# Four raw weight buffers shared by two phases, first loads of the channel mixer issued inside mixing, and two token differences on VectorE

## The chip, the core and the metric

The kernel runs on one core of a Trainium2 chip. The time is that of the device in microseconds, from the first to the last instruction, as the median of several runs. The engines work in parallel, each through its own list of instructions, and meet only at semaphores: TensorE (PE, matmuls), VectorE (DVE), ScalarE (ACT), GpSimd (POOL) and SyncE (SP), which here only issues transfers between device memory and the on-chip memory.

## What is computed

One layer of a transformer in float32 on 2048 tokens of width 1024. The change lies in its second half, which starts when the outputs of the two groups of attention heads, `o_dsa` and `o_nsa`, are in device memory:

```
mixed = jnp.concatenate([group_rms(o_dsa), group_rms(o_nsa)], axis=-1) * mix_gain
h = layer_norm(ALPHA * x + mixed @ w_out, ln1_g, ln1_b)
ffn = (jax.nn.silu(h @ w_gate) * (h @ w_up)) @ w_down
return layer_norm(ALPHA * h + ffn, ln2_g, ln2_b)
```

`w_out` is 1024 x 1024, `w_gate` and `w_up` are 1024 x 2816, `w_down` is 2816 x 1024.

## The kernel before

The program runs five phases one after the other: projection, compression, attention, mixing (`mixing_phase`) and the channel mixer (`ffn_phase`). A phase ends in a barrier of all engines, which SP reaches when its last stores have landed; the next phase uses the same on-chip memory for other tiles.

Every float32 product is made of three: an operand is split into a high part (a copy by ScalarE into a reduced format, `w_hi`, `x_hi`, `ot_hi`) and a low part (raw minus high, by VectorE, `w_lo`, `x_lo`, `ot_lo`), and TensorE adds hi x hi, hi x lo and lo x hi.

**Mixing** takes 16 tiles of 128 tokens. For a tile, ScalarE squares the attention output `o_in` (`square`), GpSimd makes the inverse root (`rinv`), VectorE scales (`scale`, which multiplies by the gain too), TensorE turns the tile (`turn_o`), ScalarE and VectorE split it (`high`, `low`), and TensorE multiplies it with `w_out` (`project`, 48 matmuls of 512 columns). VectorE adds `x` (`add_x`) and takes the moments, then come GpSimd's root, ScalarE's `norm`, VectorE's `gains`, GpSimd's addition of the offset (`add_b`, L1927, into `ho`), TensorE's `turn_h` and ScalarE's `copy_h`. SP stores `ho` to `h` and the turned tile to `h_t` (`store`). `o_in`, `x_in`, `ho` and `ht` have two buffers each; `add_b` of tile t waits until the store of tile t - 2 has landed. Tile 0 is special: its products follow the eight row blocks of `w_out` as they are split (`follow_weights`), and these come through two raw buffers, `w_raw`: the load of block k waits for w_lo of block k - 2. SP issues in the order in which its code is written: identity, gain, `ln_g` and `ln_b` broadcast, o tiles 0 and 1, the eight weight blocks, x tiles 0 and 1, o tile 2. VectorE and TensorE wait for all four of the small loads at their start.

**The channel mixer** multiplies by a scheme with 7 products in place of 8 for each 2 x 2 blocks (`ORDER = 7`), over two groups of 1024 tokens. A set n is the 7 products of two blocks of 128 columns of `w_gate` (even n) or `w_up` (odd n). The weight operands are raw blocks or sums of them in `st` (`sums`, four per set, on GpSimd), and the x operands are raw blocks or differences of them (`turn_x`, numbers 0 to 3, each in halves r = 0 and 1). The x operands are made once per group. For group 0 the blocks lie in `gs` (block 0), `y` (blocks 1 and 3, and 2 in the buffer of block 1) and the differences t2 in `lnp`. ScalarE and VectorE go through the products j = 0 to 6 in order, each with two x halves of 1024 columns and one weight part of 512, and TensorE waits for the low parts of both:

```
 for j in range(ORDER):
     for r in range(2):
         low_x(0, r, j)
     low(0, 0, j)
```

GpSimd's list at the start is: sum 0, differences 0 and 1, sums 1 and 2, difference 2, sum 3, difference 3. A product j uses: x block 0 and raw weights (j = 0), difference 1 and sum 2 (1), difference 2 and sum 1 (2), difference 0 and sum 0 (3), x block 2 (4), difference 3 (5), x block 3 and sum 3 (6). SP's first requests are the weights of set 0, x blocks 0, 1 and 3, the weights of set 1, and, once x_lo has gone through three products, x block 2 into the buffer that block 1 had.

## Time and profile before

| | us |
|---|---|
| median of 3 runs | 3850.33 (3845.58 to 3852.93) |
| the profiled execution | 3852.21 |
| its span, first to last instruction | 3850.4 |
| TensorE busy in it | 3510.7 (91%) |
| VectorE busy | 2376.6 (62%) |
| ScalarE busy | 1796.1 (47%) |
| GpSimd busy | 1251.5 (33%) |
| mixing starts | 2205.0 |
| channel mixer starts | 2460.8 |

Times in the trace count from the start of the span. A timeline lists instructions in order of time, with neighbours of one kind merged (x2, x8) and, in brackets, how long the engine was idle before and which instruction or transfer ended that. A duration given for merged instructions is that of all of them together. The granted clock is the share of TensorE's full clock, 2.4 GHz, that it had.

### The profile page before, as it was taken

How to read it: one execution, taken by the hardware profiler on the slowest of the kernel's cores; microseconds unless marked ns; L12 is line 12 of the kernel's file. 1: busy time of each engine (PE TensorE's matmuls, PEld its weight loads, DVE VectorE, ACT ScalarE, POOL GpSimd, SP SyncE). 2: the span in 40 equal slices, each digit the busy share in tenths (PEclk: the TensorE clock that was granted, in tenths of full speed). 3: DMA queues.
4: the chain of work that ended last, by engine and by line, in shares of the span. 5: the costliest groups of instructions: out<-in, count | busy, mean ns of one | idle time of the engine just before them, and what ended most of it. 6: DMA issues, size and time to landing. Idle time of an engine off the chain costs nothing. (4 is left out here: it accounts for less than half of the span.)

```text
span 3850.4 us, 55869 instructions
## 1 busy us (share of the span) xinstructions
PE 3510.7 (91%) x19064; PEld 2999.8 (78%) x19064; DVE 2376.6 (62%) x5054; ACT 1796.1 (47%) x3061; POOL 1251.5 (33%) x1951
## 2 busy tenths in 40 slices
PE   6999757989898999999989889599999999999997
PEld 6999646878787888888868768478888888888876
DVE  9999245666666667766774244476564666666354
ACT  3333125666666776776677333233332333333232
POOL 5454024444443333323322023433231235332031
PEclk9999769999999999999899989799999999999998
DMA  4343220000000000000000045332224452322344
GB/s 145 117 144 120 70 52 27 24 17 16 16 16 16 16 13 11 9 14 5 7 9 4 34 154 163 131 110 80 92 81 148 166 178 77 110 99 85 140 142 148
DMA packets 189764, 289.62 MB, mean 75 GB/s; under 512 B 33458, under 2 KB 129842, under 8 KB 189490
## 3 DMA queue, kind: packets, MB, share of 16 engines
q1 hardware_dynamic: 188004, 283.97, 22.0%
q8 instruction: 150, 2.46, 0.3%
q10 hardware_dynamic: 1488, 2.20, 0.2%
q14 instruction: 122, 1.00, 0.1%
HBM read 211.15 MB, written 74.97 MB: 74 GB/s over the span
## 5 line engine op out<-in xcount | busy, mean ns | idle before, releaser
L1459 ACT ACTIVATE a_p_t<-a_ps_st 128x512 f32<-128x512 f32 x716 | 437.7, 615 | 370.8 <-PE a_ps_st L1349 192.3
L2482 PE MATMUL f_ps<-f_x_hi,f_w_hi 128*128 128x512 f32 x1232 | 482.7, 392 | 37.2 <-DVE f_w_lo L2603 37.2
L1466 ACT ACTIVATE a_junk_a<-a_index,a_tk 128x384 bf16<-128x384 f32 (+13 forms) x336 | 445.2, 1325 | 112.2 <-DVE a_halves L1576 56.1
L2482 PE MATMUL f_ps<-f_x_lo,f_w_hi 128*128 128x512 f32 x1232 | 481.8, 391 | 0.0
L2482 PE MATMUL f_ps<-f_x_hi,f_w_lo 128*128 128x512 f32 x1232 | 481.6, 391 | 0.0
L1375 PEld LDWEIGHTS a_ps_o<-a_vsl,a_p_t 128*128 128x128 f32 x2176 | 316.9, 210 | 25.4 <-DVE a_fin L1673 2.3
L1180 POOL TENSOR_SCALAR a_tk<-a_tk,a_halves 128x1 f32<-128x1 f32 x336 | 104.0, 309 | 630.0 <-ACT a_junk_a L1466 628.8
L1375 PE MATMUL a_ps_o<-a_vsl,a_p_t 128*128 128x65 f32 x2176 | 299.9, 285 | 1.4 <-DVE a_fin L1673 1.4
L2482 PEld LDWEIGHTS f_ps<-f_x_hi,f_w_hi 128*128 128x128 f32 x1232 | 232.9, 189 | 87.5 <-DVE f_w_lo L2603 39.2
L1375 PEld LDWEIGHTS a_ps_o<-a_dv,a_p_t 128*128 128x128 f32 x2176 | 288.6, 193 | 8.8
L2502 PE MATMUL f_ps<-f_w_hi 128*128 128x512 f32 x704 | 275.1, 391 | 4.8 <-DVE f_w_lo L2613 4.8
L2502 PE MATMUL f_ps<-f_w_lo,f_w_hi 128*128 128x512 f32 x704 | 274.2, 389 | 0.0
L2502 PE MATMUL f_ps<-f_w_hi,f_w_lo 128*128 128x512 f32 x704 | 274.0, 389 | 0.0
L1375 PE MATMUL a_ps_o<-a_dv,a_p_t 128*128 128x65 f32 x2176 | 272.8, 269 | 0.0
L289 PE MATMUL p_ps<-pw_hi,px_hi 128*128 128x384 f32 (+1 forms) x672 | 228.0, 339 | 47.0 <-DVE pw_lo L395 29.5
L2482 PEld LDWEIGHTS f_ps<-f_x_hi,f_w_lo 128*128 128x128 f32 x1232 | 232.7, 189 | 48.9
L2482 PEld LDWEIGHTS f_ps<-f_x_lo,f_w_hi 128*128 128x128 f32 x1232 | 232.8, 189 | 48.0
L2609 DVE TENSOR_TENSOR f_w_lo<-f_raw,f_w_hi 128x1024 fp32r<-128x1024 f32 x88 | 121.3, 1378 | 240.7 <-ACT f_w_hi L2537 240.7
L2527 ACT ACTIVATE f_w_hi<-f_st 128x512 fp32r<-128x512 f32 x176 | 110.7, 632 | 309.7 <-PE f_ps L2482 293.9
L2537 ACT ACTIVATE f_w_hi<-f_raw 128x1024 fp32r<-128x1024 f32 x88 | 93.4, 1061 | 330.7 <-PE f_ps L2502 316.9
L1556 DVE SCALAR_TENSOR_TENSOR a_index<-a_relu,a_iw,a_index 128x512 f32<-128x512 f32 (+3 forms) x266 | 179.7, 716 | 97.3 <-ACT a_relu L1453 95.0
L289 PE MATMUL p_ps<-pw_lo,px_hi 128*128 128x384 f32 (+1 forms) x672 | 225.8, 336 | 0.0
(327 smaller groups left out, 8467.1 us busy)
## 6 DMA issues: line engine op xcount, KB each, us to landing
f_raw<-in_w_down SPq DMA_DIRECT2D x88, 512.0 KB, 3.3
px_raw<-in_x_t SPq DMA_DIRECT2D x48, 512.0 KB, 4.4
f_raw<-in_w_gate SPq DMA_DIRECT2D x44, 512.0 KB, 4.7
f_raw<-in_w_up SPq DMA_DIRECT2D x44, 512.0 KB, 4.5
g_scratch<-f_gs SPq DMA_DIRECT2D x22, 1024.0 KB, 7.5
f_raw<-g_scratch SPq DMA_DIRECT2D x88, 256.0 KB, 3.4
z_scratch<-p_z SPq DMA_DIRECT2D x16, 768.0 KB, 3.4
o_scratch<-a_oacc SPq DMA_DIRECT2D x32, 256.0 KB, 2.1
```

The lines of the kernel that those rows point to most:

```text
L289: mm = pe.matmul(bank[n % 8][:, 0:w], xs[:, j, k * P:(k + 1) * P], ws[:, j, k, 0:w], start=(k == 0 and i == 0), stop=(j not in (0, 3) and ...
L1180: last = mine(pool.tensor_scalar(moved, cnt, (t + 1) * P - 2 * TOPK + 0.5, halves[:, m:m + 1], ALU.is_le, ALU.mult))
L1375: mm = pe.matmul(ps_o[n % 2][:, h * cols:(h + 1) * cols], p_t[:, s % PT_RING, h * P:(h + 1) * P], v, start=(j == 0 and h == 0), stop=(j == ...
L1459: act.activation(p_t[:, s % PT_RING, :], ps_st[s % ST_BANKS][:, :], ACT.Exp, scale=SCALE).then_inc(exp_done, 1)
L1466: act.activation(junk_a[:, 0:w], index[t % 2][:, 0:w], ACT.Sign, bias=thr, scale=-1.0, accum_out=cnt).then_inc(counted, 1)
L1556: dve.scalar_tensor_tensor(dst, relu[:, r % RELU_RING, 0:w], weight, dst, ALU.mult, ALU.add).then_inc(index_done, 1)
L2482: mm = pe.matmul(out[:, :], w[:, j, k * P:(k + 1) * P], x[:, j, k], start=(k == 0 and i == 0), stop=(k == 3 and i == 2))
L2502: mm = pe.matmul(acc(G, a)[:, :], x[:, s + 2, cols], w[:, s + half, :], start=(f == 0 and i == 0), stop=(f == FT - 1 and i == 2))
L2527: act.activation(slot(w_hi, j), source(m, j), ACT.Copy).then_inc(hi_done, 1)
L2537: act.activation(w_hi[:, s:s + 2], raw[:, 2 * (F % 2)].rearrange("p (a n) -> p a n", a=2), ACT.Copy).then_inc(hi_done, 1)
L2609: dve.tensor_tensor(w_lo[:, s:s + 2], raw[:, 2 * (F % 2)].rearrange("p (a n) -> p a n", a=2), w_hi[:, s:s + 2].bitcast(F32), ALU.subtract) ...
```

## The change

The four raw weight buffers of the channel mixer (`raw`), its buffers `gs` and `y`, and the semaphores of their loads are now made before mixing and held through both phases. Mixing uses the four `raw` buffers for `w_out` in place of its own two; the load of block k waits for w_lo of block k - 4. SP's first requests in mixing come in another order, and the waits for small loads are parted in two: gain and identity, and the two layer norm vectors.

At mixing's step 13 of 16, SP issues seven requests of the channel mixer: the weights of sets 0 and 1, and x blocks 0, 1 and 3, each x block as one transfer of 1 MB where there were two. Their tiles of `h_t` are 0 to 7, whose stores SP waits for. The mixer's phase itself requests only x block 2 at its start, into `uu`, with no wait.

In the channel mixer the differences 0 and 1 of group 0 are made by VectorE, after its part for j = 0, and GpSimd starts with sums 0, 1 and 2. No matmul and no split is added or removed.

```diff
-        w_raw = sb("m_w_raw", [P, 2, D_MODEL])
...
-            for dst, src in ((ident, ident_in), (gain_b, gain.broadcast_to([P, D_MODEL])),
-                             (g_b, ln_g.broadcast_to([P, D_MODEL])), (b_b, ln_b.broadcast_to([P, D_MODEL]))):
-                sp.dma_start(dst[:, :], src).then_inc(small_ld, 16)
+            def load_w(k):
+                if k >= 4:
+                    sp.wait_ge(w_lo_done, k - 3)
+                sp.dma_start(raw[:, k % 4], w_rows[k]).then_inc(w_ld[k % 4], 16)
+
             for t in range(2):
                 load_o(t, t)
-            for k in range(KT):
-                if k >= 2:
-                    sp.wait_ge(w_lo_done, k - 1)
-                sp.dma_start(w_raw[:, k % 2], w_rows[k]).then_inc(w_ld[k % 2], 16)
-            for t in range(2):
-                load_x(t, t)
-
+            for dst, src in ((ident, ident_in), (gain_b, gain.broadcast_to([P, D_MODEL]))):
+                sp.dma_start(dst[:, :], src).then_inc(gain_ld, 16)
+            for k in range(3):
+                load_w(k)
+            load_x(0, 0)
+            load_w(3)
             load_o(2, 0)
+            load_w(4)
+            load_x(1, 1)
+            load_w(5)
+            for dst, src in ((g_b, ln_g.broadcast_to([P, D_MODEL])), (b_b, ln_b.broadcast_to([P, D_MODEL]))):
+                sp.dma_start(dst[:, :], src).then_inc(small_ld, 16)
+            for k in range(6, KT):
+                load_w(k)
...
+                if isinstance(t, int) and t == TILES - 3:
+                    for b in range(2):
+                        sp.wait_ge(ht_out[b], 16 * (GROUP // P // 2))
+                    for dst, src, landed in ffn_first:
+                        sp.dma_start(dst, src).then_inc(landed, 16)
...
-            pe.wait_ge(small_ld, 64)
+            pe.wait_ge(gain_ld, 32)
...
-                act.wait_ge(w_ld[k % 2], 16 * (k // 2 + 1))
-                act.activation(w_hi[:, k], w_raw[:, k % 2], ACT.Copy).then_inc(w_hi_done, 1)
+                act.wait_ge(w_ld[k % 4], 16 * (k // 4 + 1))
+                act.activation(w_hi[:, k], raw[:, k % 4], ACT.Copy).then_inc(w_hi_done, 1)
...
-                dve.wait_ge(small_ld, 64)
+                dve.wait_ge(small_ld, 32)
...
-            dve.wait_ge(small_ld, 64)
+            dve.wait_ge(gain_ld, 32)
...
+def ffn_first_loads(h_t, w_gate, w_up, raw, gs, y, raw_ld, x_ld):
+    w_cols = [w.rearrange("(k p) n -> p k n", p=P) for w in (w_gate, w_up)]
+    xt_rows = h_t.rearrange("(k p) n -> p k n", p=P)
+
+    def weights(m, half):
+        return raw[:, 2 * m + half].rearrange("p (k n) -> p k n", k=4), w_cols[m][:, 4 * half:4 * half + 4, 0:2 * P], raw_ld[2 * m + half]
+
+    def tokens(dst, n):
+        return dst, xt_rows[:, 4 * (n // 2):4 * (n // 2) + 4, (n % 2) * PART:(n % 2 + 1) * PART], x_ld[n]
+
+    return [weights(0, 0), tokens(gs[:, :, :], 0), weights(0, 1), tokens(y[:, 0:2].rearrange("p t (k n) -> p (t k) n", k=2), 1),
+            tokens(y[:, 2:4].rearrange("p t (k n) -> p (t k) n", k=2), 3), weights(1, 0), weights(1, 1)]
...
-                late = y[:, r, :].rearrange("p (k n) -> p k n", k=2)
-                return (gs[:, ks], late, late, y[:, 2 + r, :].rearrange("p (k n) -> p k n", k=2),
+                return (gs[:, ks], y[:, r, :].rearrange("p (k n) -> p k n", k=2), uu[:, 2 + 2 * r:4 + 2 * r], y[:, 2 + r, :].rearrange("p (k n) -> p k n", k=2),
...
-                for part in ((0, 1) if G == 0 else (r,)):
-                    sp.dma_start(x_blocks(G, part)[block_no], xt_rows[:, k0 + 2 * part:k0 + 2 * part + 2, col:col + PART]).then_inc(x_ld[block_no], 16)
+                if G == 0:
+                    sp.dma_start(uu[:, 2:6], xt_rows[:, k0:k0 + 4, col:col + PART]).then_inc(x_ld[block_no], 16)
+                else:
+                    sp.dma_start(x_blocks(G, r)[block_no], xt_rows[:, k0 + 2 * r:k0 + 2 * r + 2, col:col + PART]).then_inc(x_ld[block_no], 16)
...
-            load_set(0, 0)
-            for block_no in (0, 1, 3):
-                load_x(0, None, block_no)
-            load_set(0, 1)
-            sp.wait_ge(x_lo_done, 6)
             load_x(0, None, 2)
...
+        def turn_x(eng, G, r, n):
+
+            b11, b12, b21, b22, t2 = x_blocks(G, r)
+            ld = 16 * (1 if G == 0 else 2 + r)
+            if n == 0:
+                eng.wait_ge(x_ld[1], ld)
+                eng.wait_ge(x_lo_done, x_number(G, r, 0) + 1)
+                op = eng.tensor_tensor(b11, b12, b11, ALU.subtract)
+            elif n == 1:
+                eng.wait_ge(x_ld[3], ld)
+                eng.wait_ge(t_done, t_number(G, r, 0) + 1)
+                op = eng.tensor_tensor(t2, b22, b11, ALU.subtract)
+            elif n == 2:
+                eng.wait_ge(t_done, t_number(G, 1 if G == 0 else r, 1) + 1)
+                op = eng.tensor_tensor(b12, b22, b12, ALU.subtract)
+            else:
+                eng.wait_ge(x_ld[2], ld)
+                eng.wait_ge(x_lo_done, x_number(G, r, 1) + 1)
+                op = eng.tensor_tensor(t2, b21, t2, ALU.subtract)
+            op.then_inc(t_done, 1)
...
-            sums(0, 0, (0,))
+            sums(0, 0, (0, 1, 2))
             for r in range(2):
-                turn_x(0, r, 0)
-            for r in range(2):
-                turn_x(0, r, 1)
-            sums(0, 0, (1, 2))
-            for r in range(2):
-                turn_x(0, r, 2)
+                turn_x(pool, 0, r, 2)
             sums(0, 0, (3,))
             for r in range(2):
-                turn_x(0, r, 3)
+                turn_x(pool, 0, r, 3)
...
+                if j == 0:
+                    for n in range(2):
+                        for r in range(2):
+                            turn_x(dve, 0, r, n)
```

On SP at the start of mixing (`m_` names are mixing's tiles, `f_` names the channel mixer's, `m_o_in` an attention tile, `m_x_in` an x tile, `in_w_out` the weights), before:

```order
L1880 DMA m_ident<-in_consts 128x128
L1880 DMA m_gain<-in_gain 128x1024
L1880 DMA m_ln_g<-in_ln_g 128x1024
L1880 DMA m_ln_b<-in_ln_b 128x1024
L1866 DMA m_o_in<-o_scratch 128x1024 x2
L1886 DMA m_w_raw<-in_w_out 128x1024 x2
L1886 DMA m_w_raw<-in_w_out 128x1024 [waits m_w_lo_done] x6
L1870 DMA m_x_in<-in_x 128x1024 x2
L1866 DMA m_o_in<-o_scratch 128x1024 [waits m_scaled] x2
```

and in the changed kernel:

```order
L1867 DMA m_o_in<-o_scratch 128x1024 x2
L1887 DMA m_ident<-in_consts 128x128
L1887 DMA m_gain<-in_gain 128x1024
L1882 DMA f_raw<-in_w_out 128x1024 x3
L1871 DMA m_x_in<-in_x 128x1024
L1882 DMA f_raw<-in_w_out 128x1024
L1867 DMA m_o_in<-o_scratch 128x1024 [waits m_scaled]
L1882 DMA f_raw<-in_w_out 128x1024 [waits m_w_lo_done]
L1871 DMA m_x_in<-in_x 128x1024
L1882 DMA f_raw<-in_w_out 128x1024 [waits m_w_lo_done]
L1897 DMA m_ln_g<-in_ln_g 128x1024
L1897 DMA m_ln_b<-in_ln_b 128x1024
```

The o tiles and the gain now stand first, and x and o tiles stand between the weight blocks, of which only the last four wait. On SP at the end of mixing and the start of the channel mixer (`h_scratch` and `ht_scratch` are `h` and `h_t`), before:

```order
L1874 DMA h_scratch<-m_ho 128x1024 [waits m_h_done]
L1876 DMA ht_scratch<-m_ht 128x8x128 [waits m_ht_done]
L1874 DMA h_scratch<-m_ho 128x1024 [waits m_h_done]
L1876 DMA ht_scratch<-m_ht 128x8x128 [waits m_ht_done]
L1769 UNCONDITIONAL_BRANCH [waits m_h_out1,m_ht_out1,m_ht_out0,m_h_out0]
L2264 UNCONDITIONAL_BRANCH [waits barrier_Pool_Activation_PE_DVE_SP_release]
L2271 DMA f_raw<-in_w_gate 128x4x256 x2
L2294 DMA f_gs<-ht_scratch 128x2x512 x2
L2294 DMA f_y<-ht_scratch 128x2x512 x4
L2271 DMA f_raw<-in_w_up 128x4x256 x2
L2294 DMA f_y<-ht_scratch 128x2x512 [waits f_x_lo_done]
L2294 DMA f_y<-ht_scratch 128x2x512
```

and now, from the store of h_t tile 12 on:

```order
L1877 DMA ht_scratch<-m_ht 128x8x128 [waits m_ht_done]
L1912 DMA f_raw<-in_w_gate 128x4x256 [waits m_ht_out1,m_ht_out0]
L1912 DMA f_gs<-ht_scratch 128x4x512
L1912 DMA f_raw<-in_w_gate 128x4x256
L1912 DMA f_y<-ht_scratch 128x4x512 x2
L1912 DMA f_raw<-in_w_up 128x4x256 x2
L1875 DMA h_scratch<-m_ho 128x1024 [waits m_h_done]
L1877 DMA ht_scratch<-m_ht 128x8x128 [waits m_ht_done]
L1875 DMA h_scratch<-m_ho 128x1024 [waits m_h_done]
L1877 DMA ht_scratch<-m_ht 128x8x128 [waits m_ht_done]
L1875 DMA h_scratch<-m_ho 128x1024 [waits m_h_done]
L1877 DMA ht_scratch<-m_ht 128x8x128 [waits m_ht_done]
```

The requests for `f_raw`, `f_gs` and `f_y` moved from behind the barrier to a place ahead of the stores of tiles 13 to 15. On GpSimd at the start of the channel mixer, before:

```order
L2375 TENSOR_TENSOR f_st<-f_raw 128x512 [waits f_raw_ld1,f_raw_ld0,f_fixed_set]
L2393 TENSOR_TENSOR f_gs<-f_y,f_gs 128x1024 [waits f_x_lo_done,f_x_ld1] x2
L2397 TENSOR_TENSOR f_lnp<-f_y,f_gs 128x1024 [waits f_t_done,f_x_ld3] x2
L2377 TENSOR_TENSOR f_st<-f_raw 128x512
L2380 TENSOR_TENSOR f_st<-f_st,f_raw 128x512 [waits f_s_done]
L2399 TENSOR_TENSOR f_y<-f_y 128x1024 x2
L2383 TENSOR_TENSOR f_st<-f_raw,f_st 128x512 [waits f_s_done,f_lo_done]
L2403 TENSOR_TENSOR f_lnp<-f_y,f_lnp 128x1024 [waits f_x_lo_done,f_x_ld2] x2
```

and in the changed kernel:

```order
L2415 TENSOR_TENSOR f_st<-f_raw 128x512 [waits f_raw_ld1,f_raw_ld0,f_fixed_set]
L2417 TENSOR_TENSOR f_st<-f_raw 128x512
L2420 TENSOR_TENSOR f_st<-f_st,f_raw 128x512 [waits f_s_done]
L2390 TENSOR_TENSOR f_y<-f_y 128x1024 [waits f_t_done] x2
L2423 TENSOR_TENSOR f_st<-f_raw,f_st 128x512 [waits f_s_done,f_lo_done]
L2394 TENSOR_TENSOR f_lnp<-f_u,f_lnp 128x1024 [waits f_x_lo_done,f_x_ld2] x2
```

The pairs on `f_gs` and the first on `f_lnp` are gone from GpSimd. They stand on VectorE now, behind its part for j = 0:

```order
L2632 TENSOR_TENSOR f_x_lo<-f_gs,f_x_hi 128x1024 [waits f_x_hi_done] x2
L2618 TENSOR_TENSOR f_w_lo<-f_raw,f_w_hi 128x512 [waits f_hi_done]
L2383 TENSOR_TENSOR f_gs<-f_y,f_gs 128x1024 [waits f_x_lo_done,f_x_ld1] x2
L2387 TENSOR_TENSOR f_lnp<-f_y,f_gs 128x1024 [waits f_t_done,f_x_ld3] x2
L2632 TENSOR_TENSOR f_x_lo<-f_lnp,f_x_hi 128x1024 [waits f_x_hi_done] x2
L2618 TENSOR_TENSOR f_w_lo<-f_st,f_w_hi 128x512 [waits f_hi_done]
```

## Rows read from the trace of the kernel before

**Rows 1.** Windows of three stretches: busy time (instructions) of each engine, granted clock, DMA share, GB/s.
```profile
2205.00:2245.00 40.00, 18.52 (x60) 13.03 (x61) 13.83 (x14) 12.62 (x19) 2.60 (x7) 0.67 0.63 223
...
2444.00:2520.00 76.00, 30.43 (x107) 23.34 (x106) 41.53 (x31) 24.81 (x32) 38.43 (x24) 0.66 0.35 119
2520.00:3850.00 1330.00, 1300.44 (x5725) 1073.55 (x5723) 768.92 (x983) 435.00 (x635) 366.51 (x269) 0.99 0.34 119
```

**Rows 2.** Timeline of the SP queue, mixing's start: start, duration, engine, line, operation, out<-in, count.
```profile
2205.00 0.34 SPq L1880 DMA_DIRECT2D m_ident<-in_consts  x1
...
2208.12 28.52 SPq L1886 DMA_DIRECT2D m_w_raw<-in_w_out  x8
...
2237.63 0.91 SPq L1866 DMA_DIRECT2D m_o_in<-o_scratch  x2
```

**Rows 3.** Transfers from 2205 to 2245 us: rate in 40 slices of 1 us; median us to landing.
```profile
GB/s 4 172 254 262 422 328 340 418 426 406 438 254 12 0 0 0 0 0 37 303 283 225 201 0 115 381 66 369 119 0 258 266 184 385 381 184 311 418 414 303
...
m_w_raw<-in_w_out SPq DMA_DIRECT2D x8, 512.0 KB, 3.3
```

**Rows 4.** Timeline, ScalarE at mixing's start; in brackets the idle time before and its releaser.
```profile
2213.84 0.63 ACT L2014 ACTIVATE m_junk<-m_o_in 128x512 f32<-128x512 f32 x1 [15.36 <-DMA m_o_in<-o_scratch]
...
2220.61 1.99 ACT L2045 ACTIVATE m_w_hi<-m_w_raw 128x1024 fp32r<-128x1024 f32 x2
...
2244.70 0.63 ACT L2014 ACTIVATE m_junk<-m_o_in 128x512 f32<-128x512 f32 x1 [4.16 <-DMA m_o_in<-o_scratch]
```

**Rows 5.** Timeline, VectorE at mixing's start.
```profile
2216.58 1.42 DVE L2067 SCALAR_TENSOR_TENSOR m_on<-m_o_in,m_rinv,m_gain 128x512 f32<-128x512 f32 x2 [14.53 <-POOL m_rinv L1934]
...
2240.58 1.23 DVE L2102 TENSOR_TENSOR m_w_lo<-m_w_raw,m_w_hi 128x1024 fp32r<-128x1024 f32 x1 [0.85 <-ACT m_w_hi L2045]
```

**Rows 6.** Timeline, TensorE where mixing's third tile is transposed.
```profile
2250.01 1.94 PE L1956 MATMUL m_t_o<-m_ident,m_on 128*128 128x128 f32 x8 [4.32 <-DVE m_ot_lo L2072]
```

**Rows 7.** Timeline of the SP queue, mixing's end and the channel mixer's start.
```profile
2427.69 0.39 SPq L1876 DMA_DIRECT2D ht_scratch<-m_ht  x1
...
2460.82 0.95 SPq L2271 DMA_DIRECT2D f_raw<-in_w_gate  x2
```

**Rows 8.** Transfers from 2460 to 2480 us: rate in 40 slices of 0.5 us.
```profile
GB/s 0 0 0 27 160 291 344 383 391 385 293 225 201 283 352 406 410 389 381 414 401 410 410 385 393 389 379 375 367 346 352 352 322 219 51 2 0 0 0 0
```

**Rows 9.** Timeline, ScalarE, then VectorE, at the channel mixer's start.
```profile
2469.80 2.00 ACT L2549 ACTIVATE f_x_hi<-f_gs 128x1024 fp32r<-128x1024 f32 x2 [12.70 <-DMA f_gs<-ht_scratch]
...
2470.88 2.36 DVE L2617 TENSOR_TENSOR f_x_lo<-f_gs,f_x_hi 128x1024 fp32r<-128x1024 f32 x2 [18.86 <-ACT f_x_hi L2549]
2473.16 2.83 DVE L2603 TENSOR_TENSOR f_w_lo<-f_raw,f_w_hi 128x512 fp32r<-128x512 f32 x1
...
2495.56 0.68 DVE L2603 TENSOR_TENSOR f_w_lo<-f_st,f_w_hi 128x512 fp32r<-128x512 f32 x1
```

**Rows 10.** Timeline, GpSimd, mixing's last addition and the channel mixer's start.
```profile
2452.10 2.34 POOL L1927 TENSOR_TENSOR m_ho<-m_hn,m_ln_b 128x1024 f32<-128x1024 f32 x1 [2.61 <-DVE m_hn L2094]
...
2466.07 1.26 POOL L2375 TENSOR_TENSOR f_st<-f_raw 128x512 f32<-128x512 f32 x1 [5.09 <-DMA f_raw<-in_w_gate]
2472.56 5.64 POOL L2393 TENSOR_TENSOR f_gs<-f_y,f_gs 128x1024 f32<-128x1024 f32 x2 [5.23 <-DMA f_y<-ht_scratch]
2478.17 4.68 POOL L2397 TENSOR_TENSOR f_lnp<-f_y,f_gs 128x1024 f32<-128x1024 f32 x2
...
2500.80 5.67 POOL L2403 TENSOR_TENSOR f_lnp<-f_y,f_lnp 128x1024 f32<-128x1024 f32 x2 [6.25 <-DMA f_y<-ht_scratch]
```

**Rows 11.** Timeline, TensorE, the channel mixer's first products.
```profile
2476.05 0.80 PE L2482 MATMUL f_ps<-f_x_hi,f_w_hi 128*128 128x512 f32 x1 [19.58 <-DVE f_w_lo L2603]
...
2509.29 0.80 PE L2482 MATMUL f_ps<-f_x_hi,f_w_hi 128*128 128x512 f32 x1 [7.11 <-DVE f_w_lo L2603]
2509.89 0.63 PE L2482 MATMUL f_ps<-f_x_lo,f_w_hi 128*128 128x512 f32 x1
2510.31 0.63 PE L2482 MATMUL f_ps<-f_x_hi,f_w_lo 128*128 128x512 f32 x1
```

## What the change will do to the time

> **What bounds the kernel now.** I read the windows by stage first [rows 1]. In the channel mixer's long stretch, 2520 to 3850 us, TensorE is busy 1300 of 1330 us at a granted clock of 0.99: nothing there can be hidden further, and the change leaves its work alone. The two stretches in front of it are different. From 2205 to 2245 us TensorE is busy 18.5 of 40 us, and from 2444 to 2520 us 30.4 of 76 us, at granted clocks of 0.67 and 0.66. Both are starts of a phase, where every engine waits for first loads and first preparations. So I ask only how much earlier the steady work of each phase begins, and carry the difference to the end of the program.
>
> Next come the timelines of the two starts. In mixing, ScalarE waits 15.36 us for the first attention tile, whose load is issued behind four others [rows 2, 4]. Then two raw buffers make each weight load wait for the VectorE subtraction that frees its buffer, so the eight loads take 28.5 us to issue [rows 2], and the eighth w_lo starts at 2240.58 and ends at 2241.8 [rows 5]. Last of all comes the load of token tile 2, issued at 2237.63 behind the weights [rows 2]; ScalarE idles 4.16 us for it until 2244.70 [rows 4], and the chain from there (root, scaling, low part) lets TensorE transpose tile 2 at 2250.01 [rows 6]. After that TensorE has only small gaps. In the channel mixer, nothing is requested before 2460.82 [rows 7]; the first x arrives at 2469.80 [rows 9]; then GpSimd works through four turned x halves, and TensorE's first product starts at 2476.05 and its last wait ends at 2509.29 [rows 11].
>
> **Part 1, the first loads of mixing.** By the transfer rates [rows 3], bytes flow after about 2206 at 250 to 430 GB/s; from 2205.0 to 2213.84 the queue brought identity, three broadcasts and the first o tile, 0.06 + 4 x 0.524 = 2.16 MB. At the 400 GB/s of the full slices a 0.524 MB transfer takes 1.3 us, and 3.3 us from issue to landing alone [rows 3], so about 2 us are fixed. From the new order I get these landings: o0 2209.3, o1 2210.5, gain 2211.5, w0 2212.8, w1 2214, w2 2215.2, x0 2216.5, w3 2217.7, o2 2219. Between the start of squaring and of scaling lie 2216.58 - 2213.84 = 2.74 us [rows 4, 5]; scaling of tile 0 then starts at 2212.05, 4.5 us earlier. The gain is there by then, and VectorE now waits only for it and the identity.
>
> **Part 2, four buffers.** The first w_hi moves by the same 4.5 us from 2220.61 [rows 4] to 2216.1. With w0 to w3 landed, ScalarE makes one each 1.0 us (two took 1.99) and VectorE one w_lo each 1.2 us [rows 4, 5]: w_lo(0) ends at 2218.4, w_lo(3) at 2221.9. The loads w4 to w7 are issued as w_lo(0) to w_lo(3) end. They land behind the interleaved x1 and the two broadcasts: w4 2221.7, w5 2224.2, w6 2227.9, w7 2229.2. That is the transfer bound: 16 tiles and the identity, 8.45 MB, at 400 GB/s take 21 us and with the fixed part end near 2229. The last w_lo ends 1.05 + 1.2 us plus a queue step later, at 2231.6, against 2241.8. TensorE finishes tile 0 at about 2233.1.
>
> **Part 3, tile 2 early.** o2 landed long ago, so ScalarE squares it right after the last w_hi (2230.4 to 2232.1), GpSimd takes the root, VectorE scales by 2234.8. The turn of tile 1 follows the weight products (2233.1 to 2234.9), its high halves end at 2235.5, its low halves at 2236.2, and TensorE turns tile 2 at 2236.3, where it did at 2250.01 [rows 6]. **Gain 13.7 us.** The 4.16 us idle for o2 is in it. The extra waits on SP (o2 between w3 and w4) are on scaled tiles that are done by then; queued behind them are only loads that I have counted.
>
> **Part 4, the mixer's first loads near mixing's end.** Seven requests are put on SP after the store of h_t tile 12, which was issued at 2427.69 [rows 7]; with everything shifted I keep the old times for this part. They carry four weight halves of 0.524 MB and three x blocks of 1.05 MB, 5.24 MB, exactly what the old start fetched. That took from 2460.82 to about 2477.4 [rows 7, 8], 16.6 us, so they land at about 2446 with the store in front. The SP wait ahead of them is for h_t stores of tiles 0 to 7, long done. What is queued behind them is the store of h tile 13; GpSimd's addition of tile 15 needs it, since it reuses that buffer, and starts at 2452.10 [rows 10]. Expected landing 2448 to 2449, so it is hidden with 3 us to spare, at no cost.
>
> **Part 5, the mixer's start.** The phase still begins at 2460.8, since the old waits on all stores stay. ScalarE no longer waits until 2469.80, GpSimd not until 2466.07 [rows 9, 10]. Block 2 of x alone is requested there, into its own buffer, lands near 2466, and is needed at 2484. It was late before: GpSimd waited 6.25 us for it until 2500.80 [rows 10], because its buffer had to be freed first.
>
> The price of each step: a 1024 column w_lo or x_lo step 1.18 us on VectorE, a 512 column one 0.62 to 0.68 [rows 9]; on GpSimd 2.34 and 1.26 [rows 10]. The two do not overlap: a 512 column subtraction took 2.83 us beside GpSimd's subtractions [rows 9], and GpSimd's pair took 5.64 us, where the next pair took 4.68 [rows 10]. I therefore lay the steps of both engines one after the other, alternating where both are ready. With this rule the old start comes out within 0.1 us of the start of the second weight set on TensorE (2519.6: 2509.29 plus one product at half clock and two at full), so I trust it.
>
> New chain: three token sums on GpSimd interleave with two x_lo and w_lo(0); first product 2468.1 (was 2476.05). The four subtractions moved to VectorE cost 4 x 1.16 = 4.6 us there and end at 2472.7; on GpSimd they took 2472.56 to 2482.85, 10.3 us [rows 10]. Then, each with GpSimd's 2.35 us steps between: w_lo(1) 2480.4, w_lo(2) 2486.9, w_lo(3) 2492.2, w_lo(4) 2497.6, w_lo(5) 2500.6, w_lo(6) 2503.5. A product of 12 matmuls lasts 12 x 0.232 = 2.8 us at the full clock [rows 1]. The last one starts at 2503.6, and the second set at 2506.3, against 2519.6. **Gain 13.3 us.** What is late next is VectorE's chain of subtractions, no longer a load.
>
> **Sum.** The profiled execution took 3852.2 us (span 3850.4), 1.9 us above the median of the three runs, 3850.3. 13.7 + 13.3 = 27.0 us off give 3825.2 in that execution, 3823.3 at the median. I take 3824, since rounding of the landings tends to come out late.
>
> **Bounds of the unknown terms.** (a) Transfer rate in mixing's start: at the 330 GB/s that I get from 5.24 MB in 16 us [rows 8], the 8.45 MB end 4.6 us later, and the gain is 9.1 instead of 13.7; above 430 GB/s no slice goes [rows 3], which gives 1.5 us more. (b) Clock: a matmul that follows idle time is spaced 0.43 us instead of 0.23 [rows 11], 2.4 us for a product. The short gaps of the new start could leave TensorE at 1.2 GHz in its last product before the steady stretch, at up to 2.4 us, or save about as much, since the 7 us gap before 2509.29 goes. (c) The four moved subtractions, if GpSimd's own step gets in between each pair: at most two steps of 2.35 us, 4.7.
>
> **Rivals.** *The transfers are the bound of mixing's start*, term (a) in full: 3824 + 5 = 3829. For it speaks that now 16 tiles want to come in 24 us; against it that slices beyond 400 GB/s stand in both windows of transfers [rows 3, 8].
>
> *The h store waits behind the early loads.* In the old start the data arrived in the order of the requests: weights for 2466.07, x for 2469.80, the next x for 2472.56 [rows 9, 10]. If 5.24 MB move at only 250 GB/s beside mixing's own traffic, they take 21 us, h tile 13 lands at about 2454, GpSimd's last addition starts 2 to 6 us late, and TensorE's last turn and the phase's end with it: 3826 to 3830. The Trainium skill, "DMA: Bandwidth & Descriptors", section "Queues, rings and completion order", says that a DMA engine consumes the descriptors of one ring in ring order; by that rule the store cannot overtake the loads at all, which speaks against this placement. The order of arrival named above agrees.
>
> *Slower than before.* The same mechanism decides it: h tile 13 would have to land later than 2452.1 + 27 = 2479 us, so that more than 51 us pass from the requests. At 100 GB/s, 5.24 MB take 52 us and the store ends at 2483: about 3860 with the block's end pushed by 31 against 27 saved, plus waits of the h_t store behind it. Nothing in the rows goes so slow over 16 us.
>
> *The change doesn't do what it says*: mixing is held elsewhere and only the mixer's start gains (3837), or the reverse. For mixing the likeliest holder is TensorE at half clock through the weight products, which would make them 2.55 us each where VectorE delivers one each 1.2: last product 2238, gain 9.
>
> **How the numbers follow.** Forecast as summed, 3818 to 3829: 0.68. Transfer bound 3829 to 3832: 0.10. Store behind the loads: 0.08. One of the starts alone, 3834 to 3843: 0.08. Something off both starts eats it, within 0.2% of before: 0.04. Slower: 0.02. 0.2% or 7.7 us is what a measurement of this kernel can tell from no change. The range 3816 to 3836 leaves out 2 in 10 at most. Faster 0.94, same 0.04, slower 0.02.
>
> **What would show it.** In the profile after: TensorE turns mixing's tile 2 at 2235 to 2238; ScalarE idles for weights once or twice, near w6; o2 causes no wait. GpSimd's last addition in mixing follows VectorE, not a DMA. In the channel mixer the first product comes 7 to 8 us after the phase's start instead of 15.2, VectorE's moved subtractions take 1.2 us each, and the last TensorE wait before the steady stretch ends 37 to 43 us after the phase's start instead of 48.5. The stretch behind it is as long as before. Wrong would be: a w_lo(7) after 2236, a wait of GpSimd for the h store, or a steady stretch that grew.

## The result, and the profile after

| | before | changed |
|---|---|---|
| median of 5 runs, us | 3851.83 (3845.58 to 3853.34) | 3825.56 (3818.74 to 3828.66) |
| profiled execution | 3852.21 | 3825.56 |
| its span | 3850.4 | 3823.8 |

The ratio is 0.9929, with a 95% interval of 0.9918 to 0.994: 26.3 us faster. The forecast was 3824, range 3816 to 3836. The total is right; its two halves are not, as the rows show, and their errors cancelled.

Windows of the changed kernel, in the columns of [rows 1]:

```profile
2205.00:2245.00 40.00, 21.85 (x85) 17.48 (x86) 18.98 (x22) 14.52 (x24) 3.85 (x13) 0.71 0.67 241
2444.00:2520.00 76.00, 54.88 (x211) 42.67 (x210) 66.40 (x60) 33.26 (x47) 39.17 (x23) 0.80 0.20 67
2507.00:3824.00 1317.00, 1286.48 (x5664) 1062.07 (x5662) 758.68 (x968) 427.42 (x622) 360.55 (x264) 0.99 0.35 119
```

TensorE is busy 21.85 of the first 40 us (18.52 before) and 54.88 us of the 76 around the mixer's start (30.43 before). In the long stretch nothing of note changed: TensorE idles 30.5 of 1317 us, before it was 29.6 of 1330. For sharper numbers I split the end of the program in two. **Mixing's length** runs from SP's first request of mixing to the first instruction of the channel mixer: 255.8 us before (2205.00 to 2460.82), 244.6 after (2205.30 to 2449.90), **11.2 less**. **The mixer's length** runs from there to the end of the span: 1389.6 before, 1373.9 after, **15.7 less**. Their sum, 26.9, is the gain in the profiled spans (26.6) but for the start of mixing, 0.3 us later.

Timelines at mixing's start, changed kernel: SP's queue, ScalarE, VectorE, TensorE (columns as in [rows 2] and [rows 4]).

SP's queue:

```profile
2205.30 0.82 SPq L1867 DMA_DIRECT2D m_o_in<-o_scratch  x2
...
2206.64 0.43 SPq L1887 DMA_DIRECT2D m_gain<-in_gain  x1
...
2214.92 0.33 SPq L1867 DMA_DIRECT2D m_o_in<-o_scratch  x1
...
2222.31 1.26 SPq L1882 DMA_DIRECT2D f_raw<-in_w_out  x2
```

ScalarE:

```profile
2208.58 0.63 ACT L2028 ACTIVATE m_junk<-m_o_in 128x512 f32<-128x512 f32 x1 [9.80 <-DMA m_o_in<-o_scratch]
...
2231.65 1.06 ACT L2059 ACTIVATE m_w_hi<-f_raw 128x1024 fp32r<-128x1024 f32 x1 [4.22 <-DMA f_raw<-in_w_out]
```

VectorE:

```profile
2213.48 2.74 DVE L2081 SCALAR_TENSOR_TENSOR m_on<-m_o_in,m_rinv,m_gain 128x512 f32<-128x512 f32 x4 [11.13 <-DMA m_gain<-in_gain]
...
2232.74 2.49 DVE L2116 TENSOR_TENSOR m_w_lo<-f_raw,m_w_hi 128x1024 fp32r<-128x1024 f32 x2 [4.05 <-ACT m_w_hi L2059]
```

TensorE:

```profile
2234.02 0.50 PE L1991 MATMUL m_y<-m_w_hi,m_ot_hi 128*128 128x512 f32 x1 [3.47 <-DVE m_w_lo L2116]
...
2238.46 1.04 PE L1970 MATMUL m_t_o<-m_ident,m_on 128*128 128x128 f32 x8
2241.16 1.07 PE L1970 MATMUL m_t_o<-m_ident,m_on 128*128 128x128 f32 x8 [1.66 <-DVE m_ot_lo L2086]
```

Compare [rows 4 to 6]. The first attention tile is squared 3.3 us after SP's first request instead of 8.8. VectorE then idles for the gain until 2213.48. ScalarE waits 4.22 us for weight block 6, TensorE 3.47 us for its low part, and tile 2 is turned at 2241.16 (2250.01 before).

At mixing's end and the mixer's start, changed kernel: SP's queue; GpSimd; VectorE; TensorE; and, from two views of transfers, the time to landing of the `h` store requested at 2425.78 and of the two early loads of `w_up`.

SP's queue:

```profile
2421.75 3.98 SPq L1912 DMA_DIRECT2D f_raw<-in_w_up  x2
2425.78 2.58 SPq L1875 DMA_DIRECT2D h_scratch<-m_ho  x1
```

GpSimd:

```profile
2441.19 2.34 POOL L1941 TENSOR_TENSOR m_ho<-m_hn,m_ln_b 128x1024 f32<-128x1024 f32 x1 [2.61 <-DVE m_hn L2108]
2449.90 0.10 POOL L2400 MEMSET f_power<- 128x1 f32 x1 [6.37 <-POOLq L1770]
...
2450.14 1.27 POOL L2415 TENSOR_TENSOR f_st<-f_raw 128x512 f32<-128x512 f32 x1
```

VectorE:

```profile
2454.62 1.74 DVE L2618 TENSOR_TENSOR f_w_lo<-f_raw,f_w_hi 128x512 fp32r<-128x512 f32 x1
2456.29 2.35 DVE L2383 TENSOR_TENSOR f_gs<-f_y,f_gs 128x1024 f32<-128x1024 f32 x2
2458.56 2.35 DVE L2387 TENSOR_TENSOR f_lnp<-f_y,f_gs 128x1024 f32<-128x1024 f32 x2
2460.90 4.51 DVE L2632 TENSOR_TENSOR f_x_lo<-f_lnp,f_x_hi 128x1024 fp32r<-128x1024 f32 x2
2465.33 2.82 DVE L2618 TENSOR_TENSOR f_w_lo<-f_st,f_w_hi 128x512 fp32r<-128x512 f32 x1
...
2486.62 0.68 DVE L2618 TENSOR_TENSOR f_w_lo<-f_raw,f_w_hi 128x512 fp32r<-128x512 f32 x1
2487.22 2.35 DVE L2632 TENSOR_TENSOR f_x_lo<-f_y,f_x_hi 128x1024 fp32r<-128x1024 f32 x2
2489.49 0.68 DVE L2618 TENSOR_TENSOR f_w_lo<-f_st,f_w_hi 128x512 fp32r<-128x512 f32 x1
```

TensorE:

```profile
2456.42 0.79 PE L2497 MATMUL f_ps<-f_x_hi,f_w_hi 128*128 128x512 f32 x1 [10.87 <-DVE f_w_lo L2618]
...
2468.20 0.80 PE L2497 MATMUL f_ps<-f_x_hi,f_w_hi 128*128 128x512 f32 x1 [7.05 <-DVE f_w_lo L2618]
...
2484.48 0.50 PE L2497 MATMUL f_ps<-f_x_hi,f_w_hi 128*128 128x512 f32 x1 [0.48 <-DVE f_w_lo L2618]
```

Transfers:

```profile
h_scratch<-m_ho SPq DMA_DIRECT2D x1, 512.0 KB, 11.1
...
f_raw<-in_w_up SPq DMA_DIRECT2D x2, 512.0 KB, 12.6
```

GpSimd's last addition of mixing follows VectorE, as before [rows 10]. The first product comes 6.5 us after the phase's start (15.2 before [rows 11]), and the last wait of TensorE before the steady stretch ends at 34.6 us (48.5 before). The moved differences are the 2.35 us pairs at 2456.29 and 2458.56.

Three of the signs named in advance were missed. Tile 2 was to be turned at 2235 to 2238 and was at 2241.16. The last wait of TensorE was to end 37 to 43 us after the phase's start and ended at 34.6. ScalarE was to idle for weights once or twice and did so for blocks 4, 5 and 6 (1.74, 2.19 and 4.22 us).

### The profile page after: what moved, and what is told of

Read it like the earlier page. It is cut to its first block and busy times, and to the rows that moved or that the text cites. A ratio compares the mean times of both kernels' runs of the same rounds, so it can differ in the third digit from the quotient of the medians.

```text
span 3823.8 us, 55866 instructions
## 1 busy us (share of the span) xinstructions
PE 3506.8 (92%) x19064; PEld 2996.7 (78%) x19064; DVE 2383.3 (62%) x5058; ACT 1796.2 (47%) x3061; POOL 1241.4 (32%) x1947
```

## The experiments

All were timed beside the kernel before. For every kernel I read the same marks from its profile; in the first five columns they count from SP's first request of mixing, in the last two from the mixer's first instruction. "Block 6 split" is where ScalarE starts on weight block 6. After "last TensorE wait ends" a different number of products of set 0 can be left to do, so that column alone does not give the gain (in `all_dve` five are left, in the changed kernel three, in `combined` one).

| kernel | scaling | block 6 split | last w_lo ends | tile 2 turned | mixing's length | last TensorE wait ends | to the end |
|---|---|---|---|---|---|---|---|
| before | 11.6 | 32.4 | 36.8 | 45.0 | 255.8 | 48.5 | 1389.6 |
| changed | 8.2 | 26.3 | 29.9 | 35.9 | 244.6 | 34.6 | 1373.9 |
| changed_again | 8.2 | 26.4 | 29.9 | 35.9 | 244.6 | 34.6 | 1373.9 |
| mix_only | 7.9 | 24.9 | 28.5 | 32.9 | 241.7 | 48.3 | 1389.7 |
| mix_only_again | 7.9 | 25.0 | 28.6 | 33.0 | 241.8 | 48.1 | 1389.6 |
| ffn_only | 11.7 | 32.4 | 37.3 | 44.5 | 255.6 | 34.6 | 1374.0 |
| buffers_only | 11.7 | 24.8 | 29.5 | 36.3 | 246.4 | 48.3 | 1389.2 |
| order_only | 7.6 | 33.0 | 37.2 | 42.5 | 251.3 | 47.9 | 1388.2 |
| ln_late | 7.5 | 22.0 | 26.4 | 30.6 | 239.5 | 34.6 | 1375.3 |
| no_preload | 8.1 | 25.7 | 29.3 | 35.2 | 243.9 | 42.1 | 1381.4 |
| pool_diffs | 7.7 | 26.1 | 29.7 | 35.6 | 244.4 | 39.1 | 1378.2 |
| all_dve | 8.0 | 25.8 | 29.4 | 35.4 | 244.2 | 22.6 | 1367.5 |
| extra_ahead | 8.0 | 25.7 | 29.3 | 35.3 | 257.8 | 34.6 | 1375.2 |
| combined | 7.7 | 23.3 | 26.9 | 31.5 | 240.4 | 35.3 | 1370.2 |

### Each half alone, and the changed kernel again

`mix_only` is the kernel before with four buffers of mixing's own (nothing is held for the mixer) and the new order of requests:

```diff
-        w_raw = sb("m_w_raw", [P, 2, D_MODEL])
+        w_raw = sb("m_w_raw", [P, 4, D_MODEL])
```

> The kernel before with the new start of mixing alone: four raw buffers of mixing's own and the new order of SP's first requests; the channel mixer as before. Theory A (the two starts are separate and their gains add): the phase of the channel mixer begins 10.9 us earlier than before, as in the changed kernel, its own start is as before (last TensorE wait 48.5 us after the phase's start), and the time is 10.9 us shorter, 0.28%. Rival (the recorded plan was right on mixing, and what the preloads cost in mixing hid it): 13.7 us shorter.

Measured: 3839.41 us, ratio 0.9964 (0.995 to 0.9978).

`ffn_only` is the changed kernel with mixing's old order, and two of the held buffers in turn:

```diff
-                if k >= 4:
-                    sp.wait_ge(w_lo_done, k - 3)
-                sp.dma_start(raw[:, k % 4], w_rows[k]).then_inc(w_ld[k % 4], 16)
+                if k >= 2:
+                    sp.wait_ge(w_lo_done, k - 1)
+                sp.dma_start(raw[:, k % 2], w_rows[k]).then_inc(w_ld[k % 2], 16)
```

> The changed kernel with mixing's old first requests and two raw buffers in use; preloads and VectorE's differences stay. Theory A: the channel mixer's last TensorE wait ends 34.6 us after the phase's start where it was 48.5, its stretch of steady work begins 16 us earlier counted from the phase's start, and the time is 15.9 us shorter than before. Rival (the recorded plan): 13.3 us shorter. Theory that the starts depend on each other: a sum with the run of mixing alone that is off 26.9 us by more than 2.

Measured: 3836.66, ratio 0.9961 (0.9947 to 0.9975). In the profiles mixing's half alone shortens mixing by 14.1 us and leaves the mixer as it was; the mixer's half alone gives its 15.6 and leaves mixing. Each half does its work where it should, and "only one of the starts gains" falls. But 14.1 and 15.6 make 29.7, and the whole change has 26.9: by the mark set above (off by more than 2) the two parts are not independent. Neither account expected for `mix_only` holds: it gained more than the 10.9 of theory A, and its 14.1 is near the rival's 13.7 for another reason, since `no_preload` below shows that the early loads cost mixing nothing. To see whether the missing 3 us are chance, the changed kernel was run again, and later `mix_only`:

> The changed kernel once more, unedited. In its first profile mixing's tile 2 was turned 35.9 us after SP's first request of the phase; with the same start alone on the old channel mixer it was 32.9. Theory V (the landing of the sixth and seventh weight block varies by 1 to 2 us from execution to execution, and the clock makes 3 us of it): this execution lies anywhere from 32.5 to 36 us, and the phase lasts 241.5 to 244.6 us. Rival (holding the mixer's buffers or its place in memory costs 3 us each time): 35.9 and 244.6 again, within 0.3.

> The start of mixing alone on the old channel mixer, once more, unedited. Four profiles of kernels that hold the channel mixer's buffers through mixing had a mixing phase of 243.9 to 244.6 us and tile 2 turned 35.2 to 35.9 us after the first request, the first run of this one 241.7 and 32.9. Theory H (holding the buffers, which moves mixing's tiles in memory, costs about 3 us): 241.7 within 0.5 again. Theory V (the landing of weight block 6 varies by 1 us between executions, and TensorE's clock turns that into 3 us): anything up to 244.6.

Measured: 3824.64, ratio 0.9938 (0.9921 to 0.9955), and for `mix_only_again`, timed once, 3840.1 beside 3854.16. Both values came back, as the rival of the one and theory H of the other have it. Each pair agrees in mixing's length within 0.15 us, so the 2.8 us between the pairs are hardly chance. Every kernel that has exactly the new order and holds the mixer's buffers through mixing splits block 6 at 25.7 to 26.4; the two without held buffers do at 24.9 and 25.0. The two groups lie further apart from block 4 to block 6: 7.9 to 8.9 us with held buffers, 7.2 without. That is 1.4 us of the changed kernel's 3.0 at tile 2. The rest, 1.6 us, is TensorE's clock. In `mix_only`, ScalarE and TensorE, where the changed kernel has 2231.65 and 2234.02:

ScalarE:

```profile
2231.19 1.06 ACT L2054 ACTIVATE m_w_hi<-m_w_raw 128x1024 fp32r<-128x1024 f32 x1 [3.15 <-DMA m_w_raw<-in_w_out]
```

TensorE:

```profile
2233.56 0.50 PE L1986 MATMUL m_y<-m_w_hi,m_ot_hi 128*128 128x512 f32 x1 [2.22 <-DVE m_w_lo L2111]
...
2236.44 1.03 PE L1965 MATMUL m_t_o<-m_ident,m_on 128*128 128x128 f32 x8
```

The 12 matmuls of blocks 6 and 7 take 2.88 us (2233.56 to 2236.44), the full clock of 2.4 GHz. In the changed kernel the same ones take 4.44 us (2234.02 to 2238.46), after 3.47 us of idling instead of 2.22. A window of the changed kernel at that place:

```profile
2234.00:2237.00 3.00, 2.98 (x9) 2.38 (x10) 1.80 (x2) 1.32 (x4) 0.89 (x2) 0.64 0.00 0
```

TensorE is busy 2.98 of 3 us at a granted clock of 0.64: most of the stretch is at 1.2 GHz. The length of the one gap does not settle it: `no_preload` had 2.22 us there too, behind a gap of 0.36, and paid as the changed kernel did (its 12 matmuls took 4.08 us, and 5.9 us lie between the last w_lo's end and tile 2's turn, where `mix_only` and `ln_late` need 4.3 to 4.4). Why block 6 lands later with held buffers, 0.7 to 1.5 us, stays open: order and bytes are the same, and the tiles' places in memory are the difference that I know of. No run put the buffers at other places, so that they are the cause is not shown.

### Buffers without order, order without buffers

`buffers_only` is the kernel before with four buffers and its old order; `order_only` has the new order and two buffers.

```diff
-        w_raw = sb("m_w_raw", [P, 2, D_MODEL])
+        w_raw = sb("m_w_raw", [P, 4, D_MODEL])
...
-                if k >= 2:
-                    sp.wait_ge(w_lo_done, k - 1)
+                if k >= 4:
+                    sp.wait_ge(w_lo_done, k - 3)
```

> The kernel before with four raw buffers in mixing and its old order of requests. Theory A1 (the waits for a free raw buffer are the cost, and the order brings little): w0 to w3 are there at once, w4 to w7 land by 2231, the last w_lo ends near 2232.5, o tile 2 lands near 2232 with no wait, and TensorE turns tile 2 at 2239 to 2241, which is 9 to 11 us earlier than 2250.0. Rival (the earlier first o tile and the early o tile 2 are the gain, 4.5 + 4.2 us): 6 us earlier or less.

> The kernel before with the new order of SP's first requests and two raw buffers. Theory A1 (buffers are the cost): each pair of weight blocks still takes a round of landing, ScalarE and VectorE of 5.6 us, and the five tiles set between them add 1.3 us each, so the last w_lo ends at 2240 or later and only the 4.2 us wait for o tile 2 is gone: tile 2 is turned 3 to 6 us earlier. Rival (the order is the gain): 8 us or more earlier.

Measured: 3843.63, ratio 0.9976 (0.9966 to 0.9985), and 3846.52, ratio 0.9983 (0.9974 to 0.9993). Mixing is 9.4 us shorter with the buffers alone and 4.5 with the order alone: the sum, 13.9, is close to the 14.1 of `mix_only`. Tile 2 is turned 8.7 us earlier with the buffers alone (9 to 11 expected, with no wait for tile 2, and there was one of 2.79) and 2.5 earlier with the order alone (3 to 6 expected). So the buffers are the larger part, as theory A1 has it, though both gains fell short of its range. Two rows of ScalarE show what each leaves: with the buffers alone (first) tile 2 is late again, with the order alone (second) the weights are.

```profile
2237.13 0.63 ACT L2014 ACTIVATE m_junk<-m_o_in 128x512 f32<-128x512 f32 x1 [2.79 <-DMA m_o_in<-o_scratch]
```

```profile
2229.66 1.06 ACT L2054 ACTIVATE m_w_hi<-m_w_raw 128x1024 fp32r<-128x1024 f32 x1 [4.33 <-DMA m_w_raw<-in_w_out]
```

### What holds the last weights: ln_late

The broadcasts of the layer norm vectors, which nothing needs before tile 0's norm, go behind the last weight blocks.

```diff
-            for dst, src in ((g_b, ln_g.broadcast_to([P, D_MODEL])), (b_b, ln_b.broadcast_to([P, D_MODEL]))):
-                sp.dma_start(dst[:, :], src).then_inc(small_ld, 16)
             for k in range(6, KT):
                 load_w(k)
+            for dst, src in ((g_b, ln_g.broadcast_to([P, D_MODEL])), (b_b, ln_b.broadcast_to([P, D_MODEL]))):
+                sp.dma_start(dst[:, :], src).then_inc(small_ld, 16)
```

> The changed kernel with the loads of the two layer norm vectors moved behind weight blocks 6 and 7. Theory T (the transfers bound mixing's start): blocks 6 and 7 land 2.6 to 3.2 us earlier, so at 22 to 24 us after SP's first request instead of 26.4 (ScalarE's start on block 6), TensorE does not sit idle for 3.5 us and keeps its full clock, tile 2 is turned at 30 to 31.5 us instead of 35.9, and the time is 2 to 5 us shorter. Rival (SP's waits for w_lo, not the bytes, set the landings): block 6 moves by less than 1 us and nothing else changes.

Measured: 3815.78, ratio 0.9913 (0.9896 to 0.9931). ScalarE and TensorE at blocks 6 and 7:

ScalarE:

```profile
2228.49 1.07 ACT L2059 ACTIVATE m_w_hi<-f_raw 128x1024 fp32r<-128x1024 f32 x1 [0.20 <-DMA f_raw<-in_w_out]
2230.52 1.06 ACT L2059 ACTIVATE m_w_hi<-f_raw 128x1024 fp32r<-128x1024 f32 x1 [0.96 <-DMA f_raw<-in_w_out]
```

TensorE:

```profile
2232.89 0.50 PE L1991 MATMUL m_y<-m_w_hi,m_ot_hi 128*128 128x512 f32 x1 [0.19 <-DVE m_w_lo L2116]
```

Block 6 follows block 5 at once, the last w_lo ends 3.6 us earlier, TensorE has a gap of 0.19 us where it had 3.47, its clock stays up (1.6 us more), and mixing is 5.1 us shorter. Theory T holds, and the rival, that SP's waits for w_lo set the landings, falls: block 6 moved by 4.3 us. How much of the forecast's miss hangs on the two broadcasts is another question, since the forecast had counted some 2.5 us for them. Between ScalarE's starts on blocks 4 and 6 lie 8.5 us in the changed kernel and 4.8 here, so they took 3.7. The three transfers that are left take 4.8 us where the forecast had 3.7, so the slow pace is not theirs alone.

The mixer's start is 1.3 us longer: the 12 matmuls of the fifth product took 4.34 us behind a wait of 2.02, where the changed kernel had 2.88 behind 0.48. By the profiles 3.8 us remain over the changed kernel. The two ratios' intervals overlap, but timed in the same round the four executions of `ln_late` (3814.27 to 3823.05) all lie below the four of the changed kernel (3823.2 to 3825.61). By the medians the gain is 8.9 us; what it has over the profiles' 3.8 is not explained.

### What the early loads are worth, and what they cost

`no_preload` issues the seven requests at the mixer's start, ahead of x block 2.

```diff
-                if isinstance(t, int) and t == TILES - 3:
-                    for b in range(2):
-                        sp.wait_ge(ht_out[b], 16 * (GROUP // P // 2))
-                    for dst, src, landed in ffn_first:
-                        sp.dma_start(dst, src).then_inc(landed, 16)
...
+            for dst, src, landed in ffn_first:
+                sp.dma_start(dst, src).then_inc(landed, 16)
             load_x(0, None, 2)
```

> The changed kernel with the seven loads issued at the start of the channel mixer instead of inside mixing; all else as changed. Theory P (the loads stand at the head of the chain and everything behind shifts with them): the first x split starts 9 us after the phase's start, the first product at 13.1 instead of 6.5, the last w_lo of set 0 ends 6.3 us later at 46.6, and the time is 6 us longer than the changed kernel's. Rival (the chain has slack that swallows the loads): 3 us or less. Mixing lasts as long as in the changed kernel: if it gets shorter by over 1 us, the early loads did cost something there.

Measured: 3830.85, ratio 0.9948 (0.9932 to 0.9964). The mixer's length grows by 7.5 us (6 expected; x block 2 stands behind the seven there, so its delay is in this too), and mixing's does not shrink for want of the loads (its rest behind tile 2's turn is 208.7 us with and without the loads). The loads cost mixing nothing.

`extra_ahead` asks how near they were to costing. It adds one copy of 5.24 MB between two places in device memory, which nothing reads, ahead of the seven requests:

```diff
+                    sp.dma_start(spare[:, :], extra_src).then_inc(extra_ld, 16)
                     for dst, src, landed in ffn_first:
```

> The changed kernel with one more transfer of 5.24 MB, from device memory to a spare place in device memory, requested just ahead of the seven early loads; nothing reads it. It doubles what stands in front of the store of h tile 13. Theory Q (transfers of one queue are worked off in order of request): that store lands some 16 us later, at about 2453 instead of 2437, GpSimd's last addition waits for it from 2441 on, and mixing gets 12 us longer. Rival (a small store overtakes or shares the engines): the addition waits 3 us or less.

Measured, timed once: 3839.27 beside 3854.16, and 14 us more than the changed kernel's 3825. SP's queue, GpSimd, and the landing of the store of tile 13:

SP's queue:

```profile
2422.20 8.68 SPq L1914 DMA_DIRECT2D f_raw<-in_w_gate  x1
...
2439.29 3.84 SPq L1914 DMA_DIRECT2D f_raw<-in_w_up  x2
2443.18 2.67 SPq L1876 DMA_DIRECT2D h_scratch<-m_ho  x1
```

GpSimd:

```profile
2453.56 2.34 POOL L1944 TENSOR_TENSOR m_ho<-m_hn,m_ln_b 128x1024 f32<-128x1024 f32 x1 [16.36 <-issue]
```

Transfers:

```profile
f_raw<-in_w_up SPq DMA_DIRECT2D x2, 512.0 KB, 11.6
...
h_scratch<-m_ho SPq DMA_DIRECT2D x1, 512.0 KB, 10.3
```

The store is requested at 2443.18 and lands 10.3 us later, at 2453.5; GpSimd's last addition starts at 2453.56, and mixing's rest grows by 13.8 us (12 expected). The row names no releaser for it; the store's landing is the event that fits. This is the rival "the store waits behind the early loads", made to happen. SP issues it 18.2 us later than in the changed kernel (counted from mixing's first request), since one request takes up to 8.68 us while the others are outstanding. But that is not what makes it late. The second `w_up` load was requested at 2440.56 and landed at 2452.2, and the store landed 1.3 us behind it. In the changed kernel that load was requested at 2423.05 and landed at 2435.7, and the store, requested at 2425.78, landed at 2436.9, 1.2 us behind it and 4.3 us ahead of the addition at 2441.19. So in both kernels the store comes in right behind the load ahead of it, at the pace of the transfers; a store requested earlier would have come in no sooner as long as that order held. Counted from mixing's first request, the 5.24 MB more move its landing by 17.4 us (231.6 to 249.0), 300 GB/s; so about 1.3 MB more would still have been free, an estimate that takes this copy's rate for other transfers. The Trainium skill, "DMA: Bandwidth & Descriptors", section "Queues, rings and completion order", has an engine consume the descriptors of a ring in ring order, though a later write may finish before an earlier one. The trace agrees on the order: in these two kernels no store landed before the loads requested ahead of it.

### Who makes the differences: pool_diffs and all_dve

`pool_diffs` gives differences 0 and 1 back to GpSimd; `all_dve` gives VectorE 2 and 3 as well, and GpSimd only the weight sums.

```diff
                 if j == 0:
-                    for n in range(2):
+                    for n in range(3):
                         for r in range(2):
                             turn_x(dve, 0, r, n)
+                if j == 1:
+                    for r in range(2):
+                        turn_x(dve, 0, r, 3)
...
-            sums(0, 0, (0, 1, 2))
...
+            sums(0, 0)
```

> The changed kernel with differences 0 and 1 back on GpSimd in the old order; the early loads stay. Theory L (the steps of both engines form one chain): four steps of 2.35 in place of 1.16 us, the last x_lo of set 0 ends 4.8 us later, 44.5 us after the phase's start instead of 39.7, and the time is 4 to 5 us longer than the changed kernel's 3825. Rival (the moved differences save the whole 10.3 us that they took on GpSimd): 10 us longer.

> The changed kernel with differences 2 and 3 on VectorE too (after its parts for j = 0 and j = 1), so that GpSimd makes the four sums alone. Theory L (VectorE and GpSimd take turns on subtractions with two operands in SBUF, and the sum of both engines' steps is the chain): four steps of 1.16 us take the place of four of 2.35, the last w_lo of set 0 ends 4.8 us earlier, 35.5 us after the phase's start instead of 40.3, and the time is 4 to 5 us shorter. Rival (the two engines overlap and VectorE is the chain alone): VectorE's list grows by 4.6 us, and the time with it.

Measured: 3830.32, ratio 0.9943 (0.9924 to 0.9961), and 3818.81, ratio 0.9921 (0.9903 to 0.9939). The mixer's length is 4.3 us longer in the one (4 to 5 expected) and 6.4 shorter in the other (4 to 5 expected: the last w_lo of set 0 ended at 34.0, not 35.5). So of the 15.7 us of the changed kernel 7.5 go when the early loads are taken away and 4.3 when the moved differences are; no run took the rest, 3.9, apart. A candidate that was not tested is x block 2, which has a buffer of its own and was waited for 6.25 us before [rows 10]. GpSimd and VectorE in `pool_diffs`, then in `all_dve`:

GpSimd:

```profile
2450.79 5.95 POOL L2383 TENSOR_TENSOR f_gs<-f_y,f_gs 128x1024 f32<-128x1024 f32 x2 [1.23 <-DVE f_x_lo L2636]
```

VectorE:

```profile
2451.70 2.82 DVE L2622 TENSOR_TENSOR f_w_lo<-f_raw,f_w_hi 128x512 fp32r<-128x512 f32 x1
```

GpSimd:

```profile
2474.90 9.69 POOL L2415 TENSOR_TENSOR f_st<-f_raw 128x512 f32<-128x512 f32 x1 [6.91 <-DVE f_w_lo L2613]
```

VectorE:

```profile
2474.74 2.35 DVE L2627 TENSOR_TENSOR f_x_lo<-f_u,f_x_hi 128x1024 fp32r<-128x1024 f32 x2
2477.01 0.68 DVE L2613 TENSOR_TENSOR f_w_lo<-f_raw,f_w_hi 128x512 fp32r<-128x512 f32 x1
2477.62 2.35 DVE L2627 TENSOR_TENSOR f_x_lo<-f_lnp,f_x_hi 128x1024 fp32r<-128x1024 f32 x2
```

A pair of differences is 2.35 us on VectorE and 4.7 to 6.6 on GpSimd, and VectorE's own steps stretch beside GpSimd's (0.68 to 2.82).

### Both together: combined

`combined` has `ln_late` and `all_dve`, and requests the gain ahead of the second attention tile:

```diff
-            for t in range(2):
-                load_o(t, t)
+            load_o(0, 0)
             for dst, src in ((ident, ident_in), (gain_b, gain.broadcast_to([P, D_MODEL]))):
                 sp.dma_start(dst[:, :], src).then_inc(gain_ld, 16)
+            load_o(1, 1)
```

> The changed kernel with the layer norm vectors loaded behind all weight blocks, the identity and the gain requested ahead of the second attention tile, and all four differences of group 0 on VectorE. If the gains add: mixing 238.5 us instead of 244.6 (239.5 with the vectors late alone, 1 more from the gain, for which VectorE waited 2 us), the channel mixer 6.4 us shorter as with all differences on VectorE, the time 12 us below the changed kernel, near 3813. If TensorE's clock falls where it waits for the last weights or behind set 0, up to 3 us of that are lost.

Measured: 3818.93, ratio 0.9905 (0.9886 to 0.9924), the lowest ratio of all, though its interval and that of `ln_late` overlap almost wholly. The two gains did not add: over the changed kernel the profiles have 4.2 us in mixing and 3.7 in the mixer, 7.9 in all, where 12 were expected and near 3813 us. VectorE at mixing's start, the gain's time to landing, and GpSimd and TensorE in the mixer:

VectorE:

```profile
2215.26 1.42 DVE L2081 SCALAR_TENSOR_TENSOR m_on<-m_o_in,m_rinv,m_gain 128x512 f32<-128x512 f32 x2 [10.66 <-DMA m_gain<-in_gain]
```

Transfers:

```profile
m_gain<-in_gain SPq DMA_DIRECT2D x1, 512.0 KB, 6.8
```

GpSimd:

```profile
2464.33 17.10 POOL L2423 TENSOR_TENSOR f_st<-f_raw,f_st 128x512 f32<-128x512 f32 x1 [10.44 <-DVE f_w_lo L2613]
```

TensorE:

```profile
2483.26 0.50 PE L2492 MATMUL f_ps<-f_x_hi,f_w_hi 128*128 128x512 f32 x1 [2.12 <-DVE f_w_lo L2613]
```

The gain needs 6.8 us to land with one tile ahead of it, as in the changed kernel with two. Scaling starts 7.7 us after the first request; `ln_late`, with the gain in its old place, had 7.5, so moving it bought nothing. The second tile is late by it: it is squared at 2216.61, 5.5 us behind the first one's 2211.08. Mixing is 240.4 us, not `ln_late`'s 239.5. In the mixer one weight sum on GpSimd took 17.10 us, and the last product waited for it; 2.8 us of `all_dve`'s gain went there.

## Why the prediction was right, and where its terms were off

The mechanism held: both starts gained, by the causes named, and the steady stretch stayed as it was. That the two lengths together gained 26.9 us for a forecast of 27.0 is luck: mixing's start fell 2.5 us short, and the mixer's gave 2.4 more.

**Mixing's start: 13.7 forecast, 11.2 measured.** Tile 2 was to be turned 31.3 us after SP's first request, and was at 35.9, 4.6 late.
- *"The gain is there by then"* failed: VectorE waited for it until 8.2 instead of 7.05, 1.1 us. The landing of 2211.5 took the gain for an ordinary 0.524 MB transfer, 4.9 us behind its request at 2206.6; it took 6.8. Block 4, whose request waits for the first w_lo, was requested 14.5 us after the first request instead of 13.4.
- *The landings of blocks 6 and 7* were the mis-sized term. Forecast 2227.9 and 2229.2; ScalarE got block 6 at 2231.65. The last w_lo ended at 29.9 instead of 26.6: 3.3 us, of which 1.1 is the gain's. The rest came between blocks 4 and 6: five transfers in 8.5 us instead of the 6.2 that 400 GB/s give. Without the two broadcasts among them (`ln_late`) the other three still took 1.6 us each, so what slowed this stretch of the queue is only in part the broadcasts, and is open.
- *The clock at the last weight products* was a term of the sum at nothing (bound (b) speaks of the mixer's last product only) and came in at 1.6 us against me, less some 0.3 us by which the path from the last w_lo to tile 2 was laid too long.
- *A term missing on the other side*: before, TensorE went at the half clock into its first ordinary tile: the turn of tile 2 took 1.94 us in [rows 6], after it takes 1.07, and mixing's rest behind it is 208.7 us instead of 210.8. The sum had 2.1 us there at nothing.
- Right was that attention tile 2 causes no wait. "Scaled tiles that are done by then" was wrong as a statement (SP waited until 2214.92), and cost nothing, since the next request had to wait for w_lo anyway.
- "Above 430 GB/s no slice goes" misreads [rows 3], which have one of 438; the 1.5 us drawn from it play no part.

So bound (a), "the transfers are the bound of mixing's start", was part of the truth, some 2.3 us of the 4.6 that it names. It did not show in the total only because the other half was mis-sized the other way.

**The mixer's start: 13.3 forecast, 15.7 measured.** The moved differences took 4.6 us, as forecast, and ended at 11.0 us after the phase's start instead of 11.9. But laying every step of the two engines one after the other charged too much: w_lo(1) was done at 18.3 instead of 19.6, and w_lo(6) at 40.3 instead of 42.7. That is the 2.4 us. (The text trusts the rule since it met the old start within 0.1 us, but shows no working for it, and the second set began at 2519.9, not 2519.6.) GpSimd had run out of ready work by then, and VectorE's last pairs went at 2.35 us with nothing between [the rows from 2486.62]. What was late last was VectorE's chain beside GpSimd's steps, as written; `all_dve`, which gives VectorE more steps and takes GpSimd's away, shows it by 6.4 us more.

**The early loads hidden, with 3 us to spare**: right, 4.3 by the profile. SP's own issuing was not counted: the requests of `w_up` took 3.98 us to issue and the store behind them 2.58, where others take 0.4 [rows 7]. It ran beside the transfers and used none of the spare. By bytes the term was right: the seven loads and the store had landed 19.3 us after the first request (2417.6 to 2436.9), where the forecast had 20 to 21.

**Rivals.** Behind the loads: did not occur, and occurs at 5.24 MB more; that the store cannot overtake the loads held in both kernels. Slower than before: nothing came near. One start only: excluded by the halves.

## What to carry to other kernels

A chain of loads at a phase's start is priced by who stands ahead of the last one needed: list, for each request, the instruction that needs it, and put behind everything else what is needed last (here two broadcasts, worth 5 us of mixing). Requests of the next phase can be issued early and free, as long as the next store that something waits for is counted as landing behind all their bytes. When two engines share a preparation chain, move the steps to the engine that does them faster, and forecast with alternation only where the other has work ready.

## What the runs showed of the hardware

- **GpSimd can be held through many of VectorE's back-to-back subtractions.** In `all_dve` one sum of 512 columns, 1.27 us alone, took 9.69 us, while VectorE ran its own pairs at 2.35; in `combined` another took 17.10, through 16 subtractions of VectorE, and ended 1.1 us after the last of them. GpSimd's spans in a trace are rough, but TensorE's last product did wait for this one. In the changed kernel the two engines took turns instead (VectorE's 0.68 became 2.82, GpSimd's pair 6.62). The Trainium skill, "SBUF — State Buffer", section "Who interferes with whom", has a VectorE instruction with two inputs in SBUF contend with a GpSimd instruction that reads SBUF, and the order of issue decide who blocks. The runs agree on the contention (0.68 to 2.82). The order of issue alone does not tell how long: in `combined` the GpSimd step waited for the one that was ahead of it and for the 15 that followed as well. In `all_dve` and `combined` the same step, at the same 16.35 us after the phase's start, took 2.20 us in the one and 17.10 in the other.
- **A request takes SP longer while large ones are outstanding.** From 0.4 us each to 3.98 for a pair of `w_up` loads, 8.68 for a 0.5 MB load behind the 5.24 MB copy. All that is queued on SP behind it waits to be issued; in `extra_ahead` that cost the store nothing, since it landed right behind the load ahead of it.
- **Transfers on SP's queue landed in the order of their requests, and a broadcast of one row to 128 partitions kept the pace of a plain tile once the queue was running.** In the kernel before, the broadcasts of gain, `ln_g` and `ln_b` were requested at 2205.39, 2205.87 and 2206.34 and landed at 2210.0, 2211.3 and 2212.6, and the first attention tile at 2213.8: 1.3 us apart each. From a view of transfers:

```profile
m_ln_g<-in_ln_g SPq DMA_DIRECT2D x1, 512.0 KB, 5.4
m_ln_b<-in_ln_b SPq DMA_DIRECT2D x1, 512.0 KB, 6.2
```

  The changed kernel had `ln_g` and `ln_b` 1.7 and 2.0 us behind the transfer ahead of each, `no_preload` 1.3 each. The gain, the first of them, was slow: 4.6 us with 0.06 MB ahead where a weight block with an empty queue takes 3.3 [rows 3], and 6.1 to 6.8 in the kernels of the new order, with one or two tiles and the identity ahead. What sets this is open.
- **TensorE's clock at a short gap.** The same 12 matmuls took 2.88 us after 2.22 us of idling and 4.44 after 3.47; in `no_preload` they took 4.08 after a gap of 2.22 too. Which of two such starts stays at 2.4 GHz could not be read from the gap before it.
